# Token halves at ten sublayer borders of a decoder trunk (stick-breaking, MLA, RWKV-7, SwiGLU) on one core

## The reference, cut to what matters

```python
D_FF = 2816
h = jnp.concatenate([meta, x], axis=1)                    # 272 tokens x 1024
for i in range(4):
    g = norm_gains[i]
    h = h + 0.5 * _rmsnorm(_swiglu(_rmsnorm(h, g[0, 0]), ffn_w_in[i, 0], ffn_w_out[i, 0]), g[0, 1])
    u = _rmsnorm(h, g[1, 0])
    m = (stick_breaking, latent_attention, rwkv7)[i % 3](u)   # layers 0, 3 | 1 | 2
    h = h + _rmsnorm(m, g[1, 1])
    h = h + 0.5 * _rmsnorm(_swiglu(_rmsnorm(h, g[2, 0]), ffn_w_in[i, 1], ffn_w_out[i, 1]), g[2, 1])
return h[:, 16:]
```

## Time and profile before

| | |
|---|---|
| median of three runs | 2532.3 us |
| profiled execution, its own time | 2529.28 us |
| its span, first to last instruction | 2527.4 us |
| mean granted TensorE clock | 0.957 |
| matmul instructions | 20494 |

### The profile page before, as it was taken

The page is one execution under the profiler, slowest core; times in us unless marked ns, Lnnn a source line. Parts: engine busy times, 40 slices in busy tenths (PEclk is TensorE's granted clock), DMA queues, the critical chain, the costliest instruction groups (busy, mean ns, idle before and its releaser), DMA issues.

```text
span 2527.4 us, 53100 instructions
## 1 busy us (share of the span) xinstructions
PE 2322.4 (92%) x20494; PEld 2265.1 (90%) x20494; DVE 1560.9 (62%) x1841; ACT 1008.5 (40%) x1420; POOL 1818.3 (72%) x853
## 2 busy tenths in 40 slices
PE   7998989998998798998999689988999999898997
PEld 7998979998998688998999588977998999888997
DVE  7963148846863337864891958637873893335982
ACT  4343344344343434343333444324343434344342
POOL 6886737886886507886888786837788788746886
PEclk9999999999998889999999689998999999999999
DMA  5563524553553304563554232013554455433553
GB/s 183 174 203 111 177 67 126 174 199 116 172 195 117 112 19 132 173 197 119 166 185 153 77 108 93 5 36 102 173 184 156 147 175 187 133 107 95 176 187 108
DMA packets 89948, 348.82 MB, mean 138 GB/s; under 512 B 9968, under 2 KB 11760, under 8 KB 89712
## 3 DMA queue, kind: packets, MB, share of 16 engines
q1 hardware_dynamic: 89840, 347.31, 43.2%
HBM read 346.22 MB, written 1.05 MB: 137 GB/s over the span
## 4 chain that ended last, share of the span: by engine, by line
PE 73%; DVE 13%; POOL 4%; ACT 4%; issue 4%; DVEq 0%; DMA 0%; ACTq 0%; SPq 0%; POOLq 0%
PE bank L295 21%; PE bank L297 21%; PE bank L296 21%; PE bank L613 3%; DVE m L1439 2%; POOL w_lo L1246 2%; DVE hid_hi L1463 2%; DVE acc L1398 2%; DVE hid L1461 1%; DVE x_lo L1391 1%; POOL x_lo L1272 1%; DVE rstd L1384 1%; ACT w_hi L870 1%; POOL h L1259 1%; PE bank L356 1%
## 5 line engine op out<-in xcount | busy, mean ns | idle before, releaser
L1246 POOL TENSOR_TENSOR w_lo<-raw,w_hi 128x1024 fp32r<-128x1024 f32 (+2 forms) x608 | 1602.4, 2660 | 604.8 <-ACT w_hi L870 583.7
L295 PE MATMUL bank<-x_hi,w_hi 128*128 128x272 f32 (+1 forms) x3380 | 993.3, 294 | 40.3 <-POOL x_lo L1272 14.2
L297 PE MATMUL bank<-x_hi,w_lo 128*128 128x272 f32 (+1 forms) x3380 | 983.2, 291 | 0.0
L296 PE MATMUL bank<-x_lo,w_hi 128*128 128x272 f32 (+1 forms) x3380 | 980.0, 290 | 0.0
L870 ACT ACTIVATE w_hi<-raw 128x1024 fp32r<-128x1024 f32 (+2 forms) x608 | 661.0, 1116 | 231.9 <-PE bank L297 209.7
L295 PEld LDWEIGHTS bank<-x_hi,w_hi 128*128 128x128 f32 x3380 | 644.7, 191 | 53.8 <-issue 36.3
L296 PEld LDWEIGHTS bank<-x_lo,w_hi 128*128 128x128 f32 x3380 | 646.5, 191 | 0.3
L297 PEld LDWEIGHTS bank<-x_hi,w_lo 128*128 128x128 f32 x3380 | 645.5, 191 | 0.0
L1465 DVE TENSOR_TENSOR hid_lo<-hid,hid_hi 128x272 f32 (+3 forms) x176 | 417.2, 2370 | 20.2
L295 PE MATMUL bank<-hid_hi,w_hi 128*128 128x272 f32 (+1 forms) x1408 | 404.8, 287 | 1.5 <-POOL w_lo L1246 1.1
L297 PE MATMUL bank<-hid_hi,w_lo 128*128 128x272 f32 (+1 forms) x1408 | 403.6, 287 | 0.0
(11 more groups left out here) (275 smaller groups left out, 2455.3 us busy)
## 6 DMA issues: line engine op xcount, KB each, us to landing
raw<-in_ffn_in SPq DMA_DIRECT2D x352, 512.0 KB, 3.5
raw<-in_ffn_out SPq DMA_DIRECT2D x128, 704.0 KB, 4.1
raw<-in_sb_in SPq DMA_DIRECT2D x48, 512.0 KB, 3.5
raw<-in_rw_in SPq DMA_DIRECT2D x24, 512.0 KB, 3.2
raw<-in_sb_out SPq DMA_DIRECT2D x16, 512.0 KB, 3.5
raw<-in_mla_out SPq DMA_DIRECT2D x8, 512.0 KB, 3.2
raw<-in_rw_lora SPq DMA_DIRECT2D x8, 512.0 KB, 4.6
raw<-in_rw_out SPq DMA_DIRECT2D x8, 512.0 KB, 3.2
```

Of the source, the lines that this page charges most:

```text
L295: nc.tensor.matmul(o, wh, xh[:, k, cols()], start=start, stop=False)
L296: nc.tensor.matmul(o, wh, xl[:, k, cols()], start=False, stop=False)
L297: last = nc.tensor.matmul(o, wl, xh[:, k, cols()], start=False, stop=stop)
L1246: nc.gpsimd.tensor_tensor(w_lo[:, s, w], raw[:, s, w], w_hi[:, s, w], ALU.subtract).then_inc(lo_ready, 1)
```

## The change

The change applies to ten of the twelve borders: six `out` products (followed twice by `q`, three times by `in`, once by `mla_in`) and four `proj` products (each followed by `in`). The border ahead of RWKV-7 and the end of the kernel stay as they are. At these ten the tokens are cut into columns 0 to 135 and 136 to 271 (from 16 on in the last layer's cut sections).

- **TensorE.** In the last round of the output product, units 0 and 1 run as before over all tokens. Units 2 and 3 run over the first half of the tokens, and then once more over the second half, into another bank (`last_round_in_halves`). The first half's sum of squares is put in after five blocks of the second pass. The next section's first round also runs twice: first half with units 0 and 1 together, then 2, then 3; second half with units 0, 1, 2, 3 in turn. The weight slots are given back only by the second pass.
- **Next norm's sum.** `acc` over all tiles, one reduction and one product with ones are replaced by squares of single half tiles on ScalarE and one plain float32 product with ones for each of them on TensorE (16 a border, `input_sum_half`).
- **ScalarE, VectorE, GpSimdE.** Scaling, residual, `x_hi` and `x_lo` are done in 8 + 8 half tiles in place of 8 whole ones. The reciprocal is written to a PSUM bank (6 or 7). GpSimdE splits units 0 and 1 of the next section ahead of the first half's residual adds, and units 2 and 3 between the two halves' adds.

```diff
+            def part(b, s, j, k, parts, sl, start, stop):
+                (xh, xl), wh, wl = parts, w_hi[:, s, P * j:P * j + P], w_lo[:, s, P * j:P * j + P]
+                nc.tensor.matmul(bank[b][:, sl], wh, xh[:, k, sl], start=start, stop=False)
+                nc.tensor.matmul(bank[b][:, sl], wh, xl[:, k, sl], start=False, stop=False)
+                return nc.tensor.matmul(bank[b][:, sl], wl, xh[:, k, sl], start=False, stop=stop)
+            def last_round_in_halves(sec, block_of, ready):
...
+                for h in range(2):
+                    for s in (2, 3):
...
+                            end = part(b, s, j, k, parts, span(h, cut), start, stop)
+                            if h == 0 and stop:
+                                end.then_inc(part_done, 1)
+                            if h == 1 and s == 2 and j == 4:
+                                sum_output_half(0, len(tiles))
+                        if h == 1:
+                            end.then_inc(unit_used, 1)
+                pending.append(len(tiles))
+            def sum_output_half(h, count):
+                sl, b = span(h, n["cut"]), 6 + h
+                pe.wait_ge(sq_free, 2 + n["sq"] - n["kept"])
+                nc.tensor.matmul(bank[b][:, sl], ones, acc[:, sl], start=True, stop=False)
+                for t in range(count):
+                    n["sqh"] += 1
+                    pe.wait_ge(sqh_ready, n["sqh"])
+                    end = nc.tensor.matmul(bank[b][:, sl], ones, sq[:, (n["sq"] + t) % 2, sl], start=False, stop=t == count - 1)
+                end.then_inc(sum_done, 1)
+            def input_sum_half(h, k, cut):
...
+                pe.wait_ge(hsq_ready, n["hsum"])
+                end = nc.tensor.matmul(bank[4 + h][:, sl], ones, m[:, k, sl], start=k == 0, stop=k == DT_ - 1)
+            def first_round_in_halves(sec, sum_cut=None):
...
+                for h in range(2):
+                    for group in (((0, 1), (2,), (3,)), ((0,), (1,), (2,), (3,)))[h]:
+                        if h == 0:
+                            for s in group:
+                                pe.wait_ge(lo_ready, sec.start + s + 1)
+                                pe.wait_ge(bank_free[s], uses[s] + 1)
+                        for k in range(DT_):
+                            if group[0] == 0:
+                                pe.wait_ge(x_ready, base + DT_ * h + k + 1)
+                            for s in group:
+                                end = part(s, s, k, k, x_parts, span(h, cut), k == 0, k == DT_ - 1)
+                                if h == 1 and k == DT_ - 1:
+                                    end.then_inc(unit_used, 1)
+                            if group[0] == 0:
+                                if h == 0 and k == 0:
+                                    sum_output_half(1, pending.pop())
+                                input_sum_half(h, k, cut if sum_cut is None else sum_cut)
@@ scalar: halved_border
+                squares(0)
+                output_root(0)
+                ahead(2)
+                tile(0, 0)
+                tile(0, 1)
+                squares(1)
+                tile(0, 2)
+                tile(0, 3)
+                output_root(1)
+                for k in range(4, DT_):
+                    tile(0, k)
+                ahead(3)
+                for k in range(DT_):
+                    tile(1, k)
@@ gpsimd: output_section
+                split_lo(after, 0, 0)
+                split_lo(after, 0, 1)
+                add_tiles(span(0, n["cut"]))
+                split_lo(after, 0, 2)
+                split_lo(after, 0, 3)
+                add_tiles(span(1, n["cut"]))
@@ vector: halved_border
+                take_tiles_of(0)
+                for h in range(2):
+                    sl, b = span(h, cut), 6 + h
+                    inverse_root(bank[b], sl)
+                    for k in range(DT_):
+                        nc.vector.scalar_tensor_tensor(m[:, k, sl], m[:, k, sl], gain(layer, sub, 1, k), bank[b][:, sl], ALU.mult,
+                                                       ALU.mult).then_inc(apply_ready, 1)
+                        if h == 0 and k == 4:
+                            take_tiles_of(1)
+                        if k >= LAG:
+                            low_part(*then, k - LAG, sl)
+                    for k in range(DT_ - LAG, DT_):
+                        low_part(*then, k, sl)
+                inverse_root(xr, span(0, cut))
+                inverse_root(xr, span(1, cut))
```

More of the change, by code:

```diff
@@ L246, in build, with halved @@
         following = {s.name_key: t for s, t in zip(secs, secs[1:] + [None])}
+        def halved(sec):
+            after = following[sec.name_key]
+            return after is not None and after.name != "lora1"
+        last_tiles = lambda sec: ((7, 2, 3),) if sec.name == "out" else ((6, 2, 0), (7, 3, 1))
+        span = lambda h, cut: slice(cut if h == 0 else L // 2, L // 2 if h == 0 else L)
         def gain(layer, sub, post, j):
@@ L270, in taken, with product @@
                     pe.wait_ge(bank_free[b], uses[b] + 1)
-            def product(sec, block_of, ready, only=None, each_tile=False, first=None):
+            def product(sec, block_of, ready, only=None, each_tile=False, first=None, last=None):
                 if not only:
@@ L390, in swiglu, with output_product @@
                 n["hid"] += FT
-                product(next(take), halves, lambda s, k: pe.wait_ge(hid_ready, 2 + base + k + 1) if s < 2 else None)
-                sum_output()
+                output_product(next(take), halves, lambda s, k: pe.wait_ge(hid_ready, 2 + base + k + 1) if s < 2 else None)
+            def output_product(sec, block_of, ready, first=None):
+                if halved(sec):
+                    product(sec, block_of, ready, first=first, last=last_round_in_halves)
+                else:
+                    product(sec, block_of, ready, first=first)
+                    sum_output()
             def token_major(src, dst_tokens=(0, P, TAIL)):
@@ L463, in stick_breaking @@
                 n["cut"] = cut
-                product(next(take), whole, lambda s, k: None)
-                sum_output()
+                output_product(next(take), whole, lambda s, k: None)
             def latent_attention(cut):
@@ L806, in first @@
                                 last.then_inc(unit_used, 1)
-                product(sec, whole, lambda s, k: None, first=first)
+                output_product(sec, whole, lambda s, k: None, first=first)
             for at, layer in enumerate(layers):
@@ L851, in _ @@
                     sp.dma_start(raw[:, :, DT_ * P:CAP * P], A["masks"]).then_inc(rwc_loaded, 16)
-            sp.wait_ge(h_ready, DT_ * 3 * len(layers))
+            outputs = [sec for sec in secs if sec.name in ("out", "proj")]
+            sp.wait_ge(h_ready, sum(DT_ * (2 if halved(sec) else 1) for sec in outputs))
             sp.dma_start(out, h[:, :, META:L]).then_inc(stored, 16)
```

270 lines of the change are left out of this document (204 added, 66 removed).

## The result

The kernel after takes 2632.4 us (median of four runs, 2618.2 to 2656.8) against 2532.4 (2530.6 to 2533.1): the ratio is 1.0406, 95% interval 1.0317 to 1.0495. It is slower, as forecast, but by 4% where I said 2.4%: 40 us over the 2592, and 2 us beyond the range. The profiled execution took 2621.6 us. Unlike the kernel before, this one does not repeat itself within 0.3%: its runs lie up to 39 us apart, and the cause of that spread is part of the answer.

A forecast was written before the change was run, and what follows sets the result against it. TensorE's queue of matmuls bounds the kernel. At ten borders, 341.4 us of half matmuls plus 47.8 of sums with ones make 389.2 against 328.1 before, +61: forecast 2592 us, 2.4% slower, range 2560 to 2630.

The forecast's parts named there:

- The price of a half matmul: at the ten borders half matmuls start 0.112 us apart, paced by the weight load; 3048 of them take 341.4 us.
- The rival that was built on a hidden or quicker load: half matmul at its stream's 0.063 us, so TensorE is no bound at the borders: 2490 us; chance 0.10.
- The sums with ones: on TensorE at the ten borders, 208 half products with ones at 0.23 us each, 47.8 us, none hidden.
- The sum: the ten borders' work goes from 328.1 to 389.2 us, +61 us.
- The waits: at the ten borders TensorE stays busy, pass two covering the norm chain; slacks 1.3 to 2.7 us, 0.2 lost at `proj`.
- waits on top: GpSimdE makes unit 3 late or VectorE is held longer, 1.5 to 3 us a border: 2610 to 2625; chance 0.11.
- The clock: with no gap at the borders TensorE keeps the upper level, 2.4 GHz, all through; gain already in the 254.4 us.
- The rival on the clock: clock falls in thin stretches: a quarter of the 389 us at 1.2 GHz, +97 us, 2690 us; chance 0.04.

The follow-up runs named there:

- The run of both edits: kernel after, with each half matmul streaming its first 100 tokens twice and GpSimdE's unit 2 split moved between the fifth and sixth residual add: 2594.55 us, ratio 1.0249.

## Why the prediction was right in sign and too low in size

*The price of a half matmul* was right: 0.112 forecast, 0.11 measured at full clock, the same for 136 and 200 columns, and 0.213 at 1.2 GHz, near double, as a load paced by that clock would be. The Trainium skill, "TensorE: Matmul & The Clock Gate", section "Back-to-back issue gap", has 81 ns sustained for 128 tokens; these float32r matmuls do not reach it, and the measurement decides. The rival that was built on a hidden or quicker load is out.

*The sums with ones* were right: 0.23 each.

*The sum*: 389.2 us at full clock and without waits. An `out` border is 324 x 0.112 + 20 x 0.23 = 40.9, measured 41.9 with its wait; a `proj` one 37.3, measured 38.4; `mla_in` 35.5, measured 37.8 and, without waits, 35.50.

*The waits* failed. "Every slack is 1.3 to 2.7 us: TensorE is busy through the whole border": it waits 1.3 at `out`, 1.2 at `proj` (I had 0.2 there) and twice at `mla_in`, some 12 us in ten borders. At `out` I took `x_lo` of a half tile at under 0.3 us from a row of another operation (it takes 0.35 alone), and never asked what lies beside it. Tiles 4 to 7 of the first half run beside two splits that the change itself had put there, and take 5.61 us where 1.2 were counted. At `proj` I left out the square and the copy of the last half tiles, which lie bare behind pass two. The rival "waits on top" (1.5 to 3 a border) had one of its grounds right, that VectorE and GpSimdE slow each other; the step that it had late, unit 3, was not.

*The clock* failed, and it is the larger part. "With no gap I expect the upper level, 2.4 GHz, all through." There were gaps, and my reading of the earlier trace rows (64-token matmuls at clock 1.00) answered a question that does not decide. Those show that thin matmuls can run at the upper level; they say nothing of what follows once the level has fallen. In the profiled run one border of ten was caught: 57.06 less 41.94 is 15.1 us; a second lost 1.5. The rival on the clock had the sign, but put a quarter of the 389 us at the lower level; the falls of the profiled run cover 34 + 3.4 = 37.

Together for the profiled execution: 389.2, and 11.6 of waits (1.05 at each `out`, 0.8 to 1.1 at `proj`, 2.3 at `mla_in`), and 16.6 of clock make 417.4, as measured. The remaining 3 us lie outside the borders, where executions differ as much among themselves. The median of the kernel after is another 8 to 11 us up, by the same falls in other borders as far as the clocks tell. The run of both edits (2594.6) bounds it: 2629.1 less 2594.6 is 34.5 us for the clock and the waits that were taken out, and 7.1 us of waits are still in it, which makes 42, with 2.5 us less outside the borders, against the 37 to 40 that the forecast was short.

## What to carry to other kernels

Cutting a 272-token matmul in two costs the load of the weights once more, and at 200 or 136 columns the streaming is no longer what you pay. If you cut anyway, ask of each thin stretch two questions: can any wait fall into it or just ahead of it, and would the thin matmuls by themselves bring the clock back? And before you put work on GpSimdE beside a short chain on VectorE, look at where VectorE's operands are. A change that loses may still carry a part that wins: here one operand moved to PSUM, and one square taken apart.

## What the runs showed of the hardware

- Under half matmuls a low clock stayed low. After a gap of 7 us, whole matmuls ran at 2.4 GHz again within some 3 us; half matmuls, 0.213 us apart and with no gap, stayed at 1.2 GHz for all of 192 instructions, 41.9 us, and rose 4 us into the whole ones that followed. At 2.4 GHz the same stream held its level (167 instructions in 18.7 us at clock 1.00 in the third border, behind a wait of 1.3 us). The same loads with 200 columns streamed had the same waits and no fall. A wait of 1.3 us at the same place was followed by a fall in one `out` border of the profiled run and by none in the other four; why this one is open.
- A VectorE instruction with its operands in SBUF can be held for the whole of a GpSimdE one: `x_lo` 355 ns alone, 2467 and 2452 beside splits of 2400. A scale of 272 tokens is slowed: 873 ns on average with its divisor in SBUF, 491 with it in PSUM, beside the same adds. The Trainium skill, "SBUF — State Buffer", section "Who interferes with whom", states that a VectorE instruction with two SBUF inputs contends with a GpSimdE one that reads SBUF, and that the port pair which the two engines share is an exclusive lock. The trace agrees in both cases, and by it the wait at `out` could have been foreseen: `x_lo` reads `h` and `x_hi`, both in SBUF, and was placed beside the splits.
- Streaming 200 columns or 136 behind a float32r weight load of 128 columns is the same time, 0.11 us at full clock; 272 columns take 0.126.
